# Two-layer decoder trunk on one core: low gate products by ScalarE, and rows of U used at five to four tiles

## What is computed

```
q = einsum("bsd,de->bse", h, w_query); s1, s2 = scores against two sets of 128 keys
top 16 of each, top 16 of their sums -> e1, e2;  expert = e1 * 128 + e2;  gate = softmax(top_v)
act = gelu(einsum("td,thkd->thk", xt, expert_u[et])) * gt
y   = einsum("thk,thkd->td", act, expert_v[et])
```

## Time and profile before

| | |
|---|---|
| median of 3 runs | 3313.8 us (3308.7 to 3314.72) |
| profiled execution | 3312.34 us, of which the span is 3310.6 us |
| PE, DVE, ACT, POOL busy | 94%, 83%, 39%, 46% of the span |
| granted TensorE clock, mean | 0.973 |
| DMA | 849.16 MB, 256 GB/s over the span |

### The profile page before, as it was taken

How to read it: one execution, slowest core, us unless ns; L and a number is a source line. 1 busy time by engine, 2 the same in 40 slices (tenths; PEclk the granted TensorE clock), 3 DMA queues, 4 the chain that set the end, 5 groups by cost and what they waited for, 6 DMA issues and landing times.

```text
span 3310.6 us, 44003 instructions
## 1 busy us (share of the span) xinstructions
PE 3108.2 (94%) x15340; PEld 2686.9 (81%) x15340; DVE 2745.8 (83%) x4632; ACT 1290.8 (39%) x1910; POOL 1532.8 (46%) x880
## 2 busy tenths in 40 slices
PE   4898999999997899999899998999999988999999
PEld 3776799999996677887777667899999976788887
DVE  6677898999996788887776658998999977878887
ACT  3233334444442233333344763344444432333332
POOL 3333346666664434344333003456666654556221
PEclk9899999999998999999999999999999998999999
DMA  5633246898889999999624013258898999999996
GB/s 220 204 121 110 75 129 202 291 319 300 311 307 339 369 367 354 359 367 354 249 77 153 1 51 118 96 174 271 305 317 308 314 325 359 366 366 358 366 354 234
DMA packets 317118, 849.16 MB, mean 256 GB/s; under 512 B 26144, under 2 KB 157232, under 8 KB 314752
## 3 DMA queue, kind: packets, MB, share of 16 engines
q1 hardware_dynamic: 90448, 329.82, 28.4%
q0 software_dynamic: 74000, 268.81, 22.6%
q10 hardware_dynamic: 152480, 248.02, 20.7%
HBM read 743.78 MB, written 102.76 MB: 256 GB/s over the span
## 4 chain that ended last, share of the span: by engine, by line
PE 45%; DVE 28%; DMA 14%; issue 8%; POOL 3%; ACT 1%; ACTq 0%; POOLq 0%; DVEq 0%; SPq 0%
PE banks L944 14%; DVE u_rows L1699 9%; PE gbank L944 7%; DVE plane L1680 6%; DMA u_rows<-u_dram,row_of 6%; DVE hot L1676 6%; DMA gin<-gel_dram 3%; PE banks L904 3%; PE banks L906 3%; PE banks L905 3%; DVE stage L1690 3%; DMA ada_w<-ada_dram 2%; PE banks L924 2%; PE banks L926 2%; PE banks L925 2%
## 5 line engine op out<-in xcount | busy, mean ns | idle before, releaser
L434 POOL TENSOR_TENSOR w_lo<-raw,w_hi 128x1024 fp32r<-128x1024 f32 x339 | 829.2, 2448 | 775.3 <-ACT w_hi L497 771.2
L497 ACT ACTIVATE w_hi<-raw 128x1024 fp32r<-128x1024 f32 x613 | 647.6, 1057 | 494.2 <-PE banks L944 229.2
L924 PE MATMUL banks<-h_hi,w_hi 128*128 128x384 f32 x2048 | 690.5, 337 | 31.2 <-DVE w_lo L1667 17.0
L925 PE MATMUL banks<-h_lo,w_hi 128*128 128x384 f32 x2048 | 688.3, 336 | 0.0
L926 PE MATMUL banks<-h_hi,w_lo 128*128 128x384 f32 x2048 | 688.0, 336 | 0.0
L459 POOL DMA_INDIRECT v_rows<-v_dram,row_of x256 | 421.6, 1647 | 532.0 <-DVE fetched L1714 518.4
L451 POOL DMA_INDIRECT u_rows<-u_dram,row_of x256 | 273.8, 1069 | 440.3 <-DVE z L1699 434.1
L1699 DVE CUSTOM_DVE_ANT_0 u_rows<-u_rows,h_rows 128x1024 f32<-128x1024 f32 x256 | 410.7, 1605 | 65.2 <-DMA u_rows<-u_dram,row_of 64.8
L924 PEld LDWEIGHTS banks<-h_hi,w_hi 128*128 128x128 f32 x2048 | 387.3, 189 | 33.0 <-DVE w_lo L1667 18.3
L925 PEld LDWEIGHTS banks<-h_lo,w_hi 128*128 128x128 f32 x2048 | 387.4, 189 | 0.0
L926 PEld LDWEIGHTS banks<-h_hi,w_lo 128*128 128x128 f32 x2048 | 387.0, 189 | 0.0
(11 more groups left out here) (316 smaller groups left out, 4852.2 us busy)
## 6 DMA issues: line engine op xcount, KB each, us to landing
raw<-stream_dram SPq DMA_DIRECT2D x613, 512.0 KB
gel_dram<-gel ACTq DMA_DIRECT2D x256, 192.0 KB
g_dram<-stage ACTq DMA_DIRECT2D x16, 3072.0 KB
gates<-g_dram ACTq DMA_DIRECT2D x64, 768.0 KB
gin<-gel_dram ACTq DMA_DIRECT2D x64, 768.0 KB
ada_w<-ada_dram ACTq DMA_DIRECT2D x50, 512.0 KB, 4.8
ada_out<-ada_dram ACTq DMA_DIRECT2D x18, 512.0 KB, 4.7
ada_first<-ada_dram SPq DMA_DIRECT2D x8, 1024.0 KB, 20.0
```

The source lines that it names most:

```text
L434: pool.tensor_tensor(w_lo[:, s, :], raw[:, s, :], w_hi[:, s, :].bitcast(F32), ALU.subtract).then_inc(split_lo, 1)
L497: act.activation(w_hi[:, s, :], raw[:, s, :], ACT.Copy).then_inc(split_hi, 1)
L924: pe.matmul(out, wh, h_hi[:, k, 0:DENSE_T], start=(k == 0), stop=False)
L925: pe.matmul(out, wh, h_lo[:, k, 0:DENSE_T], start=False, stop=False)
```

## The change

ScalarE makes the low half of `plane`. VectorE's subtraction now writes `gate_lo` into SBUF, its multiply is of the high part alone (128x512), and ScalarE has a new function `low_planes(q)`: four ACTIVATEs (Copy) of 128x128, one for each token, whose scale is that token's column of `gate_lo`. It waits for `hot` of quad q and is called for q+2 right after `gates_high(q)`, ahead of the gelu; TensorE's `gate_quad` waits for it too. `rows_of(n)` becomes five rows in four tiles from tile 27 on (two rows in tiles 30, 34, 38, ...), so 126 dots lie in the U stage and two in V.

```diff
-    first = n - ROWS_FROM + max(n - U_GATED - 1, 0)
-    return range(first, min(PICKS, first + (2 if n > U_GATED else 1)))
+    return range(min(PICKS, 5 * (n - ROWS_FROM) // 4), min(PICKS, 5 * (n - ROWS_FROM + 1) // 4))
...
+    gate_lo = sb("gate_lo", [P, DENSE_T])
...
-    parts = banks[:, 2:4, NKEYS:]
+    high_part = bank[2][:, NKEYS:]
...
                 for q in quads:
                     gates_high(q)
+                    if q + 2 < QUADS:
+                        low_planes(q + 2)
...
+            def low_planes(q):
+
+                if q == 0:
+                    act.wait_ge(S("gate_lo"), past["gate_lo"] + 1)
+                act.wait_ge(S("hot"), past["hot"] + q + 1)
+                for u in range(QUAD):
+                    last = act.activation(plane[:, q % 2, u, 1, :], hot[:, q % 2, 1, u, :].bitcast(F32), ACT.Copy,
+                                          scale=gate_lo[:, QUAD * q + u:QUAD * q + u + 1])
+                last.then_inc(S("one_lo"), 1)
...
+            low_planes(0)
+            low_planes(1)
...
                 pe.wait_ge(S("one"), past["one"] + q + 1)
+                pe.wait_ge(S("one_lo"), past["one_lo"] + q + 1)
...
-            link(dve.tensor_tensor(parts[:, 1, :], misc[2][:, 0:DENSE_T], gate_hi.bitcast(F32), ALU.subtract))
+            dve.tensor_tensor(gate_lo[:], misc[2][:, 0:DENSE_T], gate_hi.bitcast(F32), ALU.subtract
+                              ).then_inc(S("gate_lo"), 1)
...
-                dve.tensor_tensor(plane[:, q % 2].rearrange("p t n e -> p n t e"),
-                                  hot[:, q % 2, 1].bitcast(F32).unsqueeze(1).to_broadcast(full),
-                                  parts[:, :, tok].unsqueeze(3).to_broadcast(full),
-                                  ALU.mult).then_inc(S("one"), 1)
+                wide = [P, QUAD, NKEYS]
+                dve.tensor_tensor(plane[:, q % 2, :, 0, :], hot[:, q % 2, 1].bitcast(F32),
+                                  high_part[:, tok].unsqueeze(2).to_broadcast(wide), ALU.mult
+                                  ).then_inc(S("one"), 1)
```

More of the change, by code:

```diff
@@ L113 @@
 COUNTS = {"scores": N_WQ, "sc": N_WQ, "ranked": N_WQ, "gate_arg": 1, "gate_exp": 1, "ex": 3, "ex_tp": 3,
-          "exT": 5, "hot": QUADS, "one": QUADS, "g_mm": QUADS, "g_hi": QUADS, "g_out": QUADS, "stored0": 16 * ((NBATCH + 1) // 2), "stored1": 16 * (NBATCH // 2), "picked": 2,
+          "exT": 5, "hot": QUADS, "one": QUADS, "one_lo": QUADS, "gate_lo": 1, "g_mm": QUADS, "g_hi": QUADS, "g_out": QUADS, "stored0": 16 * ((NBATCH + 1) // 2), "stored1": 16 * (NBATCH // 2), "picked": 2,
           "h_rows": 1, "h_copied": 1, "v_row": 16 * PICKS // V_ROWS, "dotted": PICKS, "z_gel": 2,
@@ L473, in peer @@
                     u_fetch(layer, j + U_ROWS - 1)
-            for j in range(rows_of(U_GATED).start + U_ROWS - 1, U_DOTS + U_ROWS - 1):
+            for j in range(rows_of(U_GATED).start + U_ROWS - 1, min(PICKS, U_DOTS + U_ROWS - 1)):
                 u_fetch(layer, j)
@@ L707, in peer @@
             act.wait_ge(S("exT"), past["exT"] + 3)
-            act.activation(parts[:, 0, :], gate_hi.bitcast(F32), ACT.Copy).then_inc(S("exT"), 1)
+            act.activation(high_part, gate_hi.bitcast(F32), ACT.Copy).then_inc(S("exT"), 1)
+            def low_planes(q):
[6 more added lines that the diff above has]
+                last.then_inc(S("one_lo"), 1)
             def gates_high(q):
@@ L1660, in peer @@
             dve.wait_ge(S("exT"), past["exT"] + 5)
-            link(dve.tensor_tensor(parts[:, 1, :], misc[2][:, 0:DENSE_T], gate_hi.bitcast(F32), ALU.subtract))
+            dve.tensor_tensor(gate_lo[:], misc[2][:, 0:DENSE_T], gate_hi.bitcast(F32), ALU.subtract
+                              ).then_inc(S("gate_lo"), 1)
+            dve.wait_ge(S("gate_lo"), past["gate_lo"] + 1)
             def low(t, off=0):
```

## The result

The changed kernel takes **3367.98 us** (median of 4 runs, 3360.17 to 3375.97), the kernel before 3312.16 beside it: ratio 1.0168, 95% interval 1.0139 to 1.0196. It is 56 us slower; the forecast was 80 faster. The profiled execution's span is 3371.3 us against 3310.6.

A forecast was written before the change was run, and what follows sets the result against it. TensorE, 94% busy, was taken as the bound, with about 69 us a layer lost to waits. Terms -14 - 11 - 16 + 1 = -40 a layer, -80 from 3312.3: 3232 us, own range 3195 to 3255, 8 in 10 3195 to 3290.

The forecast's parts named there:

- The loop: Tiles 27 to 116: doubled tiles break the dot, fetch, `w_lo` cycle of 4.73 us; held dots counted as nothing.
- rival A: Dots stay locked behind `w_lo`: 468 us for tiles 27 to 116, about 3316 in all, no change; 6%.
- Bursts: Batch stores delay rows in tiles 27 to 116: 0.7 us on TensorE for each of seven, 5 us a layer.
- the gated tiles: Tiles 27 to 116 of each layer: 19 us lost won back, 5 paid for batch stores, -14 (-19 to +9).
- Rival C: Late rows stop ScalarE's gelu and `w_hi` through `low_planes`: 8 us a batch store on TensorE, 3334 us; 9%.
- The products: ScalarE's four ACTIVATEs a quad take 1.26 us together (0.5 to 2.0), hidden by TensorE with 0.6 to spare.
- a shorter multiply alone gives nothing: VectorE in tiles 27 to 116: the dot would start 0.5 us earlier and be held 0.5 longer.
- The start: `low_planes(0)` and `(1)` hold the next `w_hi` and gelu some 6 us: costs 1 us a layer (0 to 3).
- The last 11 tiles: Tiles behind tile 116: 14 dots instead of 21 and less DMA, -11 us a layer (-4 to -19).
- V: Start of the V stage: 15 dots and fetches leave it, -16 us a layer (-8 to -24).

The follow-up runs named there:

- rows_alone: Kernel before with only the five rows of U to four tiles, VectorE making both halves of `plane`: 3369.4 us, ratio 1.018.
- products_alone: Changed kernel with the rows of U as before, so only ScalarE's products are new: 3310.86 us, ratio 1.0002 to the kernel before.
- products_slack: Changed kernel with the rows of before, four buffers for rows of U and fetches two rows ahead: 3259.23 us, ratio 0.9832 to the kernel before.
- before_slack: Kernel before with four buffers for rows of U and fetches two rows ahead: 3292.94 us, ratio 0.9927.
- before_spread: Kernel before with each batch store but the last in four parts of 768 KB, two tiles apart: 3302.32 us, ratio 0.9976.

## Why the prediction was wrong

**"The loop" failed.** It said that a doubled tile opens the loop, that later dots fall between the low parts, and that `w_lo` would then be paced by `w_hi`. The doubled tile's own pair is free (627.67, 628.82), and a tile or so later the loop is back: 68 dots of 112 are held. I summed VectorE's tile to 4.05 and TensorE's to 4.67 and made no such sum for GpSimd. It is 19.76 in four tiles, 4.94 a tile, once the lock lets a fetch wait for a dot: priced at 0.95, five fetches are 4.8; measured they are 7.9. The Trainium skill has this in "SBUF — State Buffer", "SBUF: two separate sides", where a GpSimd fetch can't write its descriptors while VectorE holds the shared ports. It ties that to VectorE's 2-port modes; here a dot with two SBUF inputs does it, 1.76 against 0.94. This is rival A in a weaker form: 448 with all rows in time, where A had 468 and the forecast 425.

**"Bursts" failed, and cost most.** I gave a row between 8.1 and 12.8 us from fetch to dot, with 14.3 to land, and put 0.7 us a burst on TensorE. The row has as little as 5.1. It is the second row of a doubled tile, its fetch stands behind a low part, and the three dots ahead of it come at VectorE's own pace of 3.7 us a quad (`hot` starts at 744.18, 747.86 and 751.53 in the trace of the changed kernel), not at two TensorE tiles. The second row in a tile is the larger part of this: with it and the old multiply (`rows_alone`) the least is 5.3, with the new multiply and one row a tile (`products_alone`) it is 11.6. Waits for rows are 61 us a layer, up to 9.73, where I had 6.2 as the worst. Taking late rows away gives 490.1 - 447.9 = 42 us in the first layer, so 6 a burst with seven bursts, if all of it is put down to them; that is an upper bound, since 12 us of the waits lie away from the stores and the edit also frees the fetch from the newest dot. It holds the slower matmuls behind the pauses too, for which I had no term. Of the 50.5 lost there, 42 go with late rows and 8 are GpSimd's cycle over the old loop's 439.6; against TensorE's own 417 the cycle costs 31. So the gated tiles, priced at -14, came out at +50.5.

**Rival C** had the place and nearly the price (8 us a burst, 3334), and its path was wrong: with the products behind the gelu the loss stays (3364, against 3368), and without any products too (`rows_alone`, 3369). Its 3334 also kept the loop's 19 us as a gain, which did not come.

**The products** were priced right (1.28 for 1.26; `plane` 0.69 for 0.68), and the sentence that a shorter multiply alone gives nothing held: ratio 1.0002. With slack it pays: `products_slack` is 34 us faster than `before_slack`. With five rows in four tiles it pays nothing again (3271.2 and 3270.5).

**The start** put 3.5 a layer between two gelus, not 1: I had a tile of lead for two sets of products, and they also waited 2.5 us for `hot`.

**The last 11 tiles** gave 8 and 9 of 11, **V** 13 and 18 of 16: both right. The sum of the first layer, 50.5 + 3.5 - 8 - 13 = 33, and of the second, 49.5 + 3.5 - 9 - 18 = 26, is 59 of the 60.7 by which the spans differ.

## What to carry to other kernels

Before putting more work on a slack engine, sum a tile on every engine that the new work touches, the one that issues its transfers too, and price a fetch beside the work that will then stand beside it. How much time a prefetched row has is set by the buffers and by how closely its uses can follow each other, not by the average pace: here a second use in one tile took it from 12 us to as little as 5. An edit that shortens one member of a closed loop gives nothing until the loop is opened; here that took one more buffer and a fetch that doesn't wait for the newest dot, with the shorter multiply, and together they gave 1.7% (`products_slack`, 3259.2; with spread stores 3256.0, not told apart from it), with the one row a tile of before.

## What was unexpected in the hardware

A fetch of 128 rows occupies GpSimd for 0.94 us alone and 1.76 beside a dot of VectorE that has two SBUF inputs. Where dots of the changed kernel waited for rows with no batch store in the 40 us before, the dot started 5.8 to 8.1 us after the start of the fetch; behind a store of 3 MB it was up to 15.4 (1017.20, the row fetched at 1001.80). Four stores of a quarter of that, two tiles apart, removed every wait for rows in `before_spread`.
